# Ten instead of eight expert chunks loaded ahead of each layer's first expert product

## The chip, the cores and the metric

One core of a Trainium2 chip runs the kernel. The metric is the device time of one execution in microseconds. The kernel before took 2226.64 us, the median of three runs (2225.43 to 2228.95).

## What is computed

Two blocks of two layers each, on 256 tokens of width 1024, all in float32. The first block has a mixer (attention and pooling in layer 0, a short convolution in layer 1), a post norm, an expert-choice FFN and a post norm again. The expert FFN is the part that the change touches: 16 experts, each takes the 32 tokens that want it most.

```python
def _expert_choice_ffn(u, w_router, w_g, w_u, w_d):
    b, n, _ = u.shape
    cap = CAPACITY_FACTOR * n // N_EXPERTS
    logits = jnp.einsum('bnd,de->ben', u, w_router, preferred_element_type=jnp.float32)
    aff = jax.nn.softmax(logits, axis=1)
    gate, idx = lax.top_k(aff, cap)
    bidx = jnp.arange(b)[:, None, None]
    xe = u[bidx, idx]
    hg = jnp.einsum('becd,edf->becf', xe, w_g)
    hu = jnp.einsum('becd,edf->becf', xe, w_u)
    ye = jnp.einsum('becf,efd->becd', jax.nn.silu(hg) * hu, w_d) * gate[..., None].astype(u.dtype)
    return jnp.zeros_like(u).at[bidx, idx].add(ye)
```

The second block has three branches (two kinds of attention and a recurrence), projections and a merge. It uses neither experts nor the code of the change.

## The kernel before

All weights come through one stream of chunks. `weight_stream` (L238) fixes the order: the modulation's and mixer's chunks of layer 0, its 96 expert chunks, the convolution's and modulation's chunks of layer 1, its 96 expert chunks, then the second block's. A chunk is 128 partitions by 4096 floats, 2 MB. SyncE (SP) issues them all in this order, one DMA each (L625 to L648); the expert chunks come from a Fori loop of NG = 4 turns with 3 * KD = 24 chunks a turn (L633 to L638).

Each chunk has a place. `two_block_program` (L303) plans them: at first six slots, from chunk `widened` on WIDE = 8 slots in a fixed cycle, and for the second block RING = 4. Slots 0 to 3 lie in the tile `ring`, slots 4 to 7 in the upper part of `arena` (from column EXTRA = 7840). In the cycle they follow one another as ring, arena, arena, ring, and again. The planner records for every chunk the one that held the slot before (`occupant`) and what the slot's semaphore `weights_landed` has to reach (`arrived`). PE counts every chunk that it has used up in the semaphore `used`, in order. SP waits, before it issues chunk n, until `used` has passed the chunk that held the slot. So SP runs at most eight chunks ahead of PE.

An expert layer on PE is `ffn` (L1286). Its order in a layer:

- `post_norm(l, 0)` on DVE (L1967) makes h, with the norm's gain and offset in the tile `ln`; it signals `("h", l, 0, a)` for the two halves a of the tokens.
- PE turns h and multiplies with the router's weights: the signal `("logits", l)`. Its input `ut` lies in the arena's columns 4096 to 6143.
- DVE picks the 32 tokens of each expert, PE spreads the indices.
- Four groups of four experts. In each, PE gathers tokens (L1335), multiplies with 8 chunks of the gate weights, 8 of the up weights (L1339 to L1342), transposes (L1349), multiplies with 8 chunks of the down weights, and adds into the tokens' rows (L1362). `products` does a chunk: two halves of 512 columns times four experts, each expert on its own 32 columns of PE (L1324). `streamed` (L1316) waits for the chunk's semaphore.

PE's four groups are a Fori loop (L1330), as are those of ACT (L755) and POOL (L2499); DVE's are written out.

Rooms that the change uses: `ln` (2048 floats a partition: gain and offset), which POOL fills by `ln_params` (L2482) for each of the norms; `tab2`, the tables of the first block, whose first 2048 columns are the rotary tables, used by the mixer of layer 0 alone, and a part of the pooling's band; and the arena's columns 2048 to 6143, which hold the sum `acc` (first the norm's work tile), then `ht` and `ye` of the expert groups (L437). `acc` is first written at the end of a group, `ht` after its sixteenth chunk.

For the ln parameters of a layer's second norm POOL waits (L2546, L2551):

```python
            ln_params(0, 1, S("post_dve").at("h", 0, 0, 1))
            ln_params(1, 1, S("post_dve").at("h", 1, 0, 1))
```

They stand in POOL's program behind its own loop over the groups.

Of the kernel before, what the change touches and what calls it, by code (L numbers as in the profile page):

```python
# [31 lines left out]
D = 1024  # L32
KD = D // P
E = 16
CAP = 2 * T // E
EG = 4
NG = E // EG
HALF = 512
# [3 lines left out]
RING = 4  # L42
WIDE = 8
EARLY = (0, 1, 2, 3, 6, 7)
ARENA = 24832
SLOT = 8 * HALF
CH = 64
# [141 lines left out]
class Signal:  # L189
# [5 lines left out]
    def up(self, *key):  # L195

        self.value += 1
        self.marks[key] = self.value
        return self.handle, 1
# [103 lines left out]
def two_block_program(nc, w, out, marks, order):  # L303
    number = {key: n for n, (key, _) in enumerate(order)}
    widened = number[("mod", 0, 11)]
    narrowed = number[("in", 0, "rkv", 0)]
    place, arrived, occupant, latest = [], [], [], {}
    early = len(EARLY)
    wide = [s for s in range(WIDE) if s not in EARLY] + [EARLY[(widened + i) % early] for i in range(early)]
    for n, (key, _) in enumerate(order):  # L310
        if n < widened:
            place.append(EARLY[n % early])
        elif n < narrowed:
            place.append(wide[(n - widened) % WIDE])
        else:
            if n == narrowed:
                narrow = sorted(range(RING), key=lambda s: latest[s])
            place.append(narrow[(n - narrowed) % RING])
        before = latest.get(place[n])
        occupant.append(before)  # L320
        arrived.append((arrived[before] if before is not None else 0) + 16)
        latest[place[n]] = n
    view, starts, start = {}, [], 0
    for key, shape in order:
# [6 lines left out]
    with ExitStack() as ctx:  # L331
# [6 lines left out]
        h = h_t[:, :].rearrange("p (a d) -> p a d", a=TT)  # L338
        ln_t = sb("ln", 2 * D)
# [4 lines left out]
        tab2 = sb("tab2", max(n_first, n_second))  # L344
        par = sb("par", n_par)
        small_t = sb("small", 1152)
        arena = sb("arena", ARENA)
# [36 lines left out]
        def S(name):  # L384
            if name not in signals:
                handle = ctx.enter_context(nc.semaphore(name))
                signals[name] = Signal(handle, marks.setdefault(name, {}))
            return signals[name]


        landed = [ctx.enter_context(nc.semaphore(f"weights_landed{s}")) for s in range(WIDE)]
        used = ctx.enter_context(nc.semaphore("weights_used"))
        EXTRA = 7840

        def room(n, cols):

            s = place[n]
            if s < RING:
                return ring[:, s * SLOT:s * SLOT + cols]
            return arena[:, EXTRA + (s - RING) * SLOT:EXTRA + (s - RING) * SLOT + cols]  # L400

        def slot(key, *dims):
            k, n = view[key] or (EG, D)
# [6 lines left out]
        def consumed(key):  # L410

            return used, number[key] + 1
# [212 lines left out]
        @block.sync  # L625
        def _(sp):
            n = 0
            while n < len(order):
                key, shape = order[n]
                if key[0] == "expert":  # L630
                    layer = key[1]

                    with sp.Fori(0, NG) as g:  # L633
                        for m in range(3 * KD):
                            i = n + m
                            sp.wait_ge(used, g * (3 * KD) + (i - WIDE + 1))
                            sp.dma_start(room(i, EG * D), w["experts"][layer][bass.ds(g, 1), m].rearrange("a p c -> p (a c)")
                                         ).then_inc(landed[place[i]], 16)  # L638
                    n += 3 * KD * NG
                    continue  # L640
                if occupant[n] is not None:
                    sp.wait_ge(used, occupant[n] + 1)
                elif n >= widened:
                    sp.wait_ge(*consumed(("mix_in", 2)))
                    sp.wait_ge(*S("norm_dve").at("out", ("first", 2)))
                c = shape[0] * shape[1]
                sp.dma_start(room(n, c), w["stream"][starts[n]:starts[n] + P * c].rearrange("(p c) -> p c", p=P)
                             ).then_inc(landed[place[n]], 16)  # L648
                if key == ("mix_in", 0):
                    sp.dma_start(m0["uc"].rearrange("p k t -> p (k t)"), w["ctx_t"]).then_inc(loaded("ctx_t")[0], 16)  # L650
                if key == ("mix_in", 1):
                    sp.dma_start(tab2[:, 0:n_first], w["tables_first"]).then_inc(loaded("tables_first")[0], 16)
                n += 1
            for a in range(TT):
                sp.wait_ge(*S("second_dve").at("residual", 1, a))
                sp.dma_start(out[0, a * P:(a + 1) * P], h[:, a]).then_inc(loaded("result")[0], 16)
            sp.wait_ge(*loaded("result", TT))
# [360 lines left out]
        def _(pe):  # L1018
# [267 lines left out]
            def ffn(l):  # L1286
# [3 lines left out]
                for a in range(TT):  # L1290
# [4 lines left out]
                    mm = project(bank(0)[:, a * E:(a + 1) * E], lambda k: ff["ut"][:, k, a * P:(a + 1) * P], lambda k: router[:, k])  # L1295
# [18 lines left out]
                base = number[("expert", l, 0)]  # L1314

                def streamed(g, m, k):  # L1316
                    i = base + m * KD + k
                    pe.wait_ge(landed[place[i]], g * (16 * 3 * KD // WIDE) + arrived[i])
                    return room(i, EG * D).rearrange("p (e f) -> p e f", e=EG)

                def products(b, x, k, wk):
                    for half in range(2):
                        for e in range(EG):
                            mm = M(bank(b + half)[32 * e:32 * e + 32], x[:, k, 32 * e:32 * e + 32],  # L1324
                                   wk[:, e, half * HALF:(half + 1) * HALF], start=k == 0, stop=k == KD - 1,
                                   tile_position=(0, 32 * e))
                    return mm

                Sx.open_loop()
                with pe.Fori(0, NG) as g:  # L1330

                    pe.wait_ge(*Spl.turn(g, "pick"))
                    for k in range(KD):
                        for a in range(TT):
                            mm = M(bank(6 + k // 4)[:, k % 4 * P:k % 4 * P + P], h[:, a, k * P:(k + 1) * P], ff["pick_g"][:, a],  # L1335
                                   start=a == 0, stop=a == 1)
                        if k % 4 == 3:
                            mm.then_inc(*Sx.up("gather", k // 4))
                    pe.wait_ge(*Sax.turn(g, "xg", 3))  # L1339
                    pe.wait_ge(*Svx.turn(g, "xg", 7))  # L1340
                    for m in range(2):
                        for k in range(KD):  # L1342
                            mm = products(2 * m, ff["xg"], k, streamed(g, m, k))
                            mm.then_inc(used, 1)
                    for b in range(2):
                        pe.wait_ge(*Svx.turn(g, "hidden", b))
                        for i in range(4):
                            k = 4 * b + i
                            mm = nc.tensor.transpose(bank(6 + b)[:, i * P:(i + 1) * P], ff["hg"][:, k * P:(k + 1) * P],  # L1349
                                                     T1("ident"))  # L1350
                        mm.then_inc(*Sx.up("turned", b))
                    for k in range(KD):
                        if k % 4 == 0:
                            pe.wait_ge(*Sax.turn(g, "ht", k // 4))
                        mm = products(4, ff["ht"], k, streamed(g, 2, k))
                        mm.then_inc(used, 1)

                    for a in range(TT):
                        for half in range(2):
                            if a == 0:  # L1360
                                pe.wait_ge(*Svx.turn(g, "ye", half))
                            M(bank(2 * a + half), ff["put_g"][:, a * P:(a + 1) * P], ff["ye"][:, half * HALF:(half + 1) * HALF],  # L1362
                              start=True, stop=True).then_inc(*Sx.up("y", a, half))
                Sx.close_loop(NG)

            def second(l):
# [1104 lines left out]
        def _(po):  # L2471
# [10 lines left out]
            def ln_params(l, part, last):  # L2482
                if last is not None:
                    po.wait_ge(*last)
                for i, n in enumerate(("ln_mix_g", "ln_mix_b") if part == 0 else ("ln_ffn_g", "ln_ffn_b")):
                    po.dma_start(ln[:, i], w[n][l:l + 1, :].to_broadcast([P, D])).then_inc(loaded("ln")[0], 16)
# [56 lines left out]
            router(0)  # L2543
            gate_bias(1, 0)
            ffn(0)
            ln_params(0, 1, S("post_dve").at("h", 0, 0, 1))  # L2546
            gate_bias(1, 1)
            ln_params(1, 0, S("post_dve").at("h", 0, 1, 1))
            router(1)
            ffn(1)  # L2550
            ln_params(1, 1, S("post_dve").at("h", 1, 0, 1))  # L2551
            second(0)
            second(1)

# [45 lines left out]
```

## Time and profile before

| | |
|---|---|
| median of 3 runs | 2226.64 us (2225.43 to 2228.95) |
| the profiled execution | 2229.26 us, its span 2227.5 us |
| mean granted TensorE clock | 0.900 |
| PE busy, of the span | 1773.7 us (80%) |
| DVE, ACT, POOL busy | 569.0, 357.9, 57.6 us |
| moved by DMA | 586.61 MB, mean 263 GB/s |
| expert chunks | 192 of 2048 KB, issued by SP at L637 |

The span runs from the first to the last instruction of the program; the device time is 1.8 us longer. Busy times are sums over instructions. "PE" is the matmuls, "PEld" the weight loads, "SPq" the DMAs issued by SP. A timeline row merges instructions of one line: its start, the time to the end of the last one, the count behind x, and in brackets the idle time before it with what ended it. The x2 of a timeline row of SPq covers two issues; the second begins 0.33 us, the time of one issue, before the row's end.

### The profile page before, as it was taken

To read this page: it belongs to the slowest core of one execution; us is meant where nothing else is said; L and a number is where in the kernel's file an instruction comes from. 1 tells how busy PE (TensorE), PEld (TensorE's weight loads), DVE (VectorE), ACT (ScalarE), POOL (GpSimd) and SP (SyncE) were. 2 spreads that over 40 slices of the span, in tenths; PEclk is the share of its full clock that TensorE was granted. 3 is DMA by queue.
4 is the path that set the end of the run, shared out by engine and by line. 5 is a ranking of instruction groups with operands and counts; after the bars stand their busy time and mean duration, and the time that the engine had idled before them with its cause. 6 is when DMAs were issued, how large, how long until landed. Compare 5 with 4: busy or idle time off the path is not lost. (4 is left out here: it accounts for less than half of the span.)

```text
span 2227.5 us, 27241 instructions
## 1 busy us (share of the span) xinstructions
PE 1773.7 (80%) x11768; PEld 1050.5 (47%) x11768; DVE 569.0 (26%) x1125; ACT 357.9 (16%) x721; POOL 57.6 (3%) x69
## 2 busy tenths in 40 slices
PE   6897765656568977656665679999999999999999
PEld 4454220211117842112111167787578678775775
DVE  0434010100007640001000035332343242414432
ACT  1231000000000010000000013313431122324310
POOL 0000000000000000000000001010000001100000
PEclk9997787888879977878787789999999999999999
DMA  9892899999999928999999943112423232113221
GB/s 405 354 381 85 353 428 428 428 428 428 428 428 425 393 102 362 428 428 428 428 428 422 428 177 144 71 61 85 151 76 114 102 135 77 71 63 118 110 91 43
DMA packets 43502, 586.61 MB, mean 263 GB/s; under 512 B 4912, under 2 KB 5040, under 8 KB 8080
## 3 DMA queue, kind: packets, MB, share of 16 engines
q1 hardware_dynamic: 40464, 574.18, 62.6%
q0 software_dynamic: 2224, 8.32, 0.9%
q10 hardware_dynamic: 720, 2.74, 0.3%
q8 instruction: 73, 1.20, 0.2%
q14 instruction: 21, 0.17, 0.0%
HBM read 584.17 MB, written 1.05 MB: 263 GB/s over the span
## 5 line engine op out<-in xcount | busy, mean ns | idle before, releaser
L1324 PE MATMUL ps<-ring,arena 128*32 128x512 f32 x1536 | 251.5, 789 | 180.2 <-DMA ring<-in_experts 167.4
L1324 PE MATMUL ps<-arena 128*32 128x512 f32 x1536 | 244.1, 771 | 154.0 <-DMA arena<-in_experts 154.0
L1090 PE MATMUL ps<-arena,ring 128*128 128x256 f32 (+3 forms) x1248 | 236.9, 351 | 9.2 <-DVE arena L1870 2.6
L1090 PEld LDWEIGHTS ps<-arena,ring 128*128 128x128 f32 (+2 forms) x1248 | 206.0, 191 | 38.5 <-ACT arena L685 6.1
L1324 PEld LDWEIGHTS ps<-ring,arena 128*32 128x32 f32 x1536 | 49.5, 128 | 362.9 <-DMA ring<-in_experts 228.0
L1324 PEld LDWEIGHTS ps<-arena 128*32 128x32 f32 x1536 | 49.1, 126 | 348.7 <-DMA arena<-in_experts 257.7
L1420 PE MATMUL ps<-arena,ring 128*128 128x256 f32 x768 | 183.5, 388 | 0.0
L1420 PEld LDWEIGHTS ps<-arena,ring 128*128 128x128 f32 x768 | 142.9, 191 | 29.1 <-issue 9.7
L1443 PE MATMUL ps<-arena,ring 128*128 128x256 f32 x640 | 152.0, 389 | 0.0
L2099 DVE TENSOR_TENSOR arena<-ps,arena 128x512 f32<-128x512 f32 x16 | 10.3, 686 | 499.4 <-PE ps L1324 499.4
L1443 PEld LDWEIGHTS ps<-arena,ring 128*128 128x128 f32 x640 | 124.1, 195 | 27.3 <-issue 10.1
L1090 PE MATMUL ps<-arena 128*128 128x256 f32 (+2 forms) x416 | 102.2, 406 | 4.5 <-ACT arena L985 2.5
L1090 PEld LDWEIGHTS ps<-arena 128*128 128x128 f32 x416 | 76.1, 196 | 30.2 <-issue 16.7
L2103 DVE TENSOR_TENSOR arena<-ps,gate 128x512 f32<-128x512 f32 x16 | 10.3, 686 | 300.0 <-PE ps L1324 300.0
L764 ACT ACTIVATE arena<-ps 128x512 f32<-128x512 f32 x16 | 9.5, 597 | 308.2 <-PE ps L1349 308.2
L758 ACT ACTIVATE arena<-ps,modcol 128x128 f32<-128x128 f32 x32 | 12.1, 457 | 277.7 <-PE ps L1335 277.7
L1743 PE MATMUL ps<-ring,ln 128*128 128x512 f32 x128 | 55.3, 592 | 0.0
L761 ACT ACTIVATE arena<-ps 128x1024 f32<-128x1024 f32 x8 | 8.2, 1024 | 221.9 <-PE ps L1324 221.9
L965 ACT ACTIVATE arena<-arena 128x128 f32<-128x128 f32 x64 | 28.6, 448 | 91.7 <-DVE arena L2413 91.7
L1055 PE MATMUL ps<-ring,arena 128*32 128x512 f32 x176 | 26.4, 734 | 20.2 <-DMA tab<-in_tables 15.8
L1090 PE MATMUL ps<-ring,arena 128*128 128x512 f32 x96 | 42.3, 593 | 0.0
L2243 DVE TENSOR_TENSOR arena<-arena,ps 128x512 f32<-128x512 f32 (+1 forms) x40 | 25.4, 635 | 61.1 <-PE ps L1542 61.0
(337 smaller groups left out, 1900.9 us busy)
## 6 DMA issues: line engine op xcount, KB each, us to landing
ring<-in_experts SPq DMA_DIRECT2D x96, 2048.0 KB, 35.6
arena<-in_experts SPq DMA_DIRECT2D x96, 2048.0 KB, 35.8
ring<-in_stream SPq DMA_DIRECT2D x61, 2048.0 KB, 8.6
arena<-in_stream SPq DMA_DIRECT2D x15, 2048.0 KB, 21.1
ring<-in_stream SPq DMA_DIRECT2D x2, 1728.0 KB, 7.0
gate<-in_b_mod POOLq DMA_DIRECT2D x4, 512.0 KB, 10.9
ring<-in_stream SPq DMA_DIRECT2D x4, 512.0 KB, 3.6
tab<-in_tables_first SPq DMA_DIRECT2D x1, 1729.0 KB, 42.5
```

The source lines that it names most:

```text
L758: A(ff["xg"][:, k], bank(6)[:, k * P:(k + 1) * P], ACT.Identity, scale=modcol[:, l, 3, k, 0:1], bias=modcol[:, l, 2, k, 0:1]).then_inc(*Sx ...
L764: A(ff["ht"][:, 4 * b:4 * b + 4], bank(6 + b).rearrange("p (k n) -> p k n", k=4), ACT.Copy).then_inc(*Sx.up("ht", b))
L965: A(at2["prob"][:, u % 2, o:o + n], at2["score"][:, u % 2, o:o + n], ACT.Exp, bias=st[:, 4 * (u % 2) + a:4 * (u % 2) + a + 1], accum_out=s ...
L1055: mm = M(bank(mod_bank((l, j)))[o:o + 32], md["condT"][:, k], slot(key)[:, k], start=k < 4, stop=k >= 4, tile_position=(0, o))
L1090: mm = M(dst, lhs(k), rhs(k), start=k == 0, stop=k == n - 1)
L1324: mm = M(bank(b + half)[32 * e:32 * e + 32], x[:, k, 32 * e:32 * e + 32], wk[:, e, half * HALF:(half + 1) * HALF], start=k == 0, stop=k == ...
L1420: mm = M(bank(fill_bank(n))[:, x * T:x * T + T], slot(key)[:, k, c:c + P], s2["ht"][:, k], start=k == 0, stop=k == KD - 1)
L1443: mm = M(bank(fill_bank(n))[:, x * T:x * T + T], slot(key)[:, k, c:c + P], s2["ht"][:, k], start=k == 0, stop=k == KD - 1)
L1743: mm = M(bank(2 * a + j), merged[:, k, a * P:(a + 1) * P], slot(key)[:, k], start=k == 0, stop=k == KD - 1)
L2099: V.tensor_tensor(ff["hg"][:, b * HALF:(b + 1) * HALF], bank(2 + b), ff["hg"][:, b * HALF:(b + 1) * HALF], ALU.mult).then_inc(*up("hidden" ...
L2103: V.tensor_tensor(ff["ye"][:, b * HALF:(b + 1) * HALF], bank(4 + b), gate[:, 1, b * HALF:(b + 1) * HALF], ALU.mult).then_inc(*up("ye", b))
L2243: V.tensor_tensor(m, m, bank(hh)[:, x * 256:], ALU.subtract).then_inc(*Sv.up("inv", *K, n, hh))
```

## The change

Two rooms are added to the eight slots, with semaphores of their own, each used once a layer. Place 8 (HALVED) takes expert chunk 8 in two halves: columns 0 to 2047 of the chunk into `ln`, 2048 to 4095 into `tab2`. Place 9 (WHOLE) takes chunk 9 into the arena's columns 2048 to 6143. The other 94 expert chunks of a layer, and all after them, go round the eight slots as before. SP waits for the second h of the layer's first post norm before chunk 8, and for the logits before chunk 9. POOL's load of the second norm's parameters waits for chunk 8 to be used. The loops over groups on SP and PE are written out, since the chunks' places are no longer the same in each turn.

```diff
+HALVED, WHOLE = WIDE, WIDE + 1
...
+        elif key[0] == "expert" and key[2] in (WIDE, WIDE + 1):
+            place.append(HALVED if key[2] == WIDE else WHOLE)
         elif n < narrowed:
-            place.append(wide[(n - widened) % WIDE])
+            place.append(wide[rounds % WIDE])
+            rounds += 1
...
-        arrived.append((arrived[before] if before is not None else 0) + 16)
+        arrived.append((arrived[before] if before is not None else 0) + (32 if place[n] == HALVED else 16))
...
-        landed = [ctx.enter_context(nc.semaphore(f"weights_landed{s}")) for s in range(WIDE)]
+        landed = [ctx.enter_context(nc.semaphore(f"weights_landed{s}")) for s in range(WIDE + 2)]
...
             s = place[n]
+            if s == WHOLE:
+                return arena[:, 2048:2048 + cols]
...
+        def halves_of(n):
+
+            return (ln_t[:, 0:2 * D], tab2[:, 0:2 * D])
...
-                if key[0] == "expert":
-                    layer = key[1]
-
-                    with sp.Fori(0, NG) as g:
-                        for m in range(3 * KD):
-                            i = n + m
-                            sp.wait_ge(used, g * (3 * KD) + (i - WIDE + 1))
-                            sp.dma_start(room(i, EG * D), w["experts"][layer][bass.ds(g, 1), m].rearrange("a p c -> p (a c)")
-                                         ).then_inc(landed[place[i]], 16)
-                    n += 3 * KD * NG
-                    continue
                 if occupant[n] is not None:
                     sp.wait_ge(used, occupant[n] + 1)
...
+                if key[0] == "expert":
+                    _, layer, s = key
+                    src = w["experts"][layer][s // (3 * KD), s % (3 * KD)]
+                    if place[n] == HALVED:
+                        sp.wait_ge(*S("post_dve").at("h", layer, 0, 1))
+                        for i, part in enumerate(halves_of(n)):
+                            sp.dma_start(part, src[:, i * 2 * D:(i + 1) * 2 * D]).then_inc(landed[HALVED], 16)
+                    else:
+                        if place[n] == WHOLE:
+                            sp.wait_ge(*S("ffn_pe").at("logits", layer))
+                        sp.dma_start(room(n, EG * D), src).then_inc(landed[place[n]], 16)
+                    n += 1
+                    continue
...
                 def streamed(g, m, k):
-                    i = base + m * KD + k
-                    pe.wait_ge(landed[place[i]], g * (16 * 3 * KD // WIDE) + arrived[i])
-                    return room(i, EG * D).rearrange("p (e f) -> p e f", e=EG)
+
+                    i = base + (3 * g + m) * KD + k
+                    pe.wait_ge(landed[place[i]], arrived[i])
+                    parts_of = halves_of(i) if place[i] == HALVED else (room(i, EG * D)[:, 0:2 * D], room(i, EG * D)[:, 2 * D:])
+                    return lambda e, f: parts_of[e // 2][:, e % 2 * D + f * HALF:e % 2 * D + (f + 1) * HALF]
...
-                with pe.Fori(0, NG) as g:
-
+                for g in range(NG):
+                    up = Sx.again if g else Sx.up
...
-            ln_params(0, 1, S("post_dve").at("h", 0, 0, 1))
+            ln_params(0, 1, consumed(("expert", 0, WIDE)))
...
-            ln_params(1, 1, S("post_dve").at("h", 1, 0, 1))
+            ln_params(1, 1, consumed(("expert", 1, WIDE)))
```

On SP, from the last chunk ahead of layer 0's experts (L647) into the loop over them, before (an ISA row is a wait):

```order
L647 DMA ring<-in_stream 128x4096 [waits weights_used]
L633 UNCONDITIONAL_BRANCH
L633 ISA
L637 ISA [waits weights_used]
L637 DMA ring<-in_experts 128x4096
L636 REGISTER_ALU
L637 ISA [waits weights_used]
L637 DMA arena<-in_experts 128x4096
```

The same place with the change, from the last chunk ahead of the experts (L659) on:

```order
L659 DMA ring<-in_stream 128x4096 [waits weights_used]
L655 DMA ring<-in_experts 128x4096 [waits weights_used]
L655 DMA arena<-in_experts 128x4096 [waits weights_used] x2
L655 DMA ring<-in_experts 128x4096 [waits weights_used] x2
L655 DMA arena<-in_experts 128x4096 [waits weights_used] x2
L655 DMA ring<-in_experts 128x4096 [waits weights_used]
L651 DMA ln<-in_experts 128x2048 [waits post_dve,norm_dve,weights_used]
L651 DMA tab<-in_experts 128x2048
L655 DMA arena<-in_experts 128x4096 [waits ffn_pe,norm_dve,weights_used]
L655 DMA ring<-in_experts 128x4096 [waits weights_used]
```

Three DMAs for the two chunks now stand behind the first eight expert chunks, ahead of the first chunk that takes over a slot from an expert chunk, and no register work is left.

On PE, the products of chunks 7 to 10 of the first group, before (L1324):

```order
L1324 MATMUL ps<-ring,arena 32x512 [waits weights_landed0]
L1324 MATMUL ps<-ring,arena 32x512 x7
L1324 MATMUL ps<-ring,arena 32x512 [waits weights_landed1]
L1324 MATMUL ps<-ring,arena 32x512 x7
L1318 REGISTER_ALU
L1324 MATMUL ps<-arena 32x512 [waits weights_landed4]
L1324 MATMUL ps<-arena 32x512 x7
```

And with the change (L1338):

```order
L1338 MATMUL ps<-ring,arena 32x512 [waits weights_landed0]
L1338 MATMUL ps<-ring,arena 32x512 x7
L1338 MATMUL ps<-ln,arena 32x512 [waits weights_landed8]
L1338 MATMUL ps<-ln,arena 32x512
L1338 MATMUL ps<-tab,arena 32x512 x2
L1338 MATMUL ps<-ln,arena 32x512 x2
L1338 MATMUL ps<-tab,arena 32x512 x2
L1338 MATMUL ps<-arena 32x512 [waits weights_landed9]
L1338 MATMUL ps<-arena 32x512 x7
L1338 MATMUL ps<-ring,arena 32x512 [waits weights_landed1]
```

Chunk 8 is read from `ln` and `tab2` by turns, chunk 9 from the arena, and chunk 10 takes the slot that chunk 8 had. The products are the same in number and shape.

## Rows read from the trace of the kernel before

**Rows 1.** Page: busy time, then tenths and GB/s in 40 slices of 55.7 us.
```profile
PE 1773.7 (80%) x11768; PEld 1050.5 (47%) x11768; DVE 569.0 (26%) x1125; ACT 357.9 (16%) x721; POOL 57.6 (3%) x69
...
PE   6897765656568977656665679999999999999999
...
DMA  9892899999999928999999943112423232113221
GB/s 405 354 381 85 353 428 428 428 428 428 428 428 425 393 102 362 428 428 428 428 428 422 428 177 144 71 61 85 151 76 114 102 135 77 71 63 118 110 91 43
```

**Rows 2.** Busy time by stretch: length, PE, PEld, DVE, ACT, POOL, PEclk, DMA share, GB/s.
```profile
165.00:228.00 63.00, 49.09 (x163) 31.58 (x161) 26.74 (x61) 9.58 (x21) 0.93 (x2) 0.76 0.21 75
228.00:246.00 18.00, 16.97 (x156) 5.17 (x160) 0.93 (x3) 1.02 (x1) 0.19 (x1) 1.00 0.79 319
246.00:671.00 425.00, 255.22 (x1536) 62.70 (x1528) 22.24 (x36) 21.34 (x30) 2.81 (x8) 0.81 1.01 428
...
699.00:777.00 78.00, 76.49 (x365) 65.96 (x363) 55.12 (x102) 2.42 (x8) 0.00 (x0) 1.00 0.99 405
777.00:840.00 63.00, 48.20 (x164) 30.31 (x164) 27.25 (x62) 9.57 (x21) 0.40 (x1) 0.78 0.28 104
...
858.00:1288.00 430.00, 256.96 (x1528) 63.12 (x1528) 22.24 (x36) 21.35 (x30) 4.90 (x12) 0.80 1.01 427
1288.00:1312.00 24.00, 15.78 (x88) 12.91 (x88) 15.01 (x28) 6.46 (x20) 0.00 (x0) 0.79 0.41 173
1312.00:1500.00 188.00, 180.86 (x2230) 152.57 (x2231) 71.59 (x115) 49.32 (x86) 22.41 (x17) 1.00 0.26 95
```

**Rows 3.** Timeline of PE in layer 0's experts: chunks 0 to 2, 10, 22, 23, 71.
```profile
228.65 1.92 PE L1324 MATMUL ps<-ring,arena 128*32 128x512 f32 x16 [1.54 <-DVE arena L2091]
230.38 3.62 PE L1324 MATMUL ps<-arena 128*32 128x512 f32 x32
233.82 3.62 PE L1324 MATMUL ps<-ring,arena 128*32 128x512 f32 x32
...
249.59 3.15 PE L1324 MATMUL ps<-arena 128*32 128x512 f32 x16 [2.98 <-DMA arena<-in_experts]
...
308.36 3.50 PE L1324 MATMUL ps<-arena 128*32 128x512 f32 x16 [2.98 <-DMA arena<-in_experts]
313.26 1.92 PE L1324 MATMUL ps<-ring,arena 128*32 128x512 f32 x16 [1.40 <-DMA ring<-in_experts]
...
548.38 1.92 PE L1324 MATMUL ps<-ring,arena 128*32 128x512 f32 x16 [1.38 <-DMA ring<-in_experts]
```

**Rows 4.** Timeline of SP's DMA issues: chunks 7 and 8 of layer 0, of layer 1.
```profile
192.14 38.96 SPq L637 DMA_DIRECT2D ring<-in_experts  x2
...
804.84 37.70 SPq L637 DMA_DIRECT2D ring<-in_experts  x2
```

**Rows 5.** Timeline of PE: chunk 95 of layer 0, of layer 1.
```profile
668.46 1.92 PE L1324 MATMUL ps<-ring,arena 128*32 128x512 f32 x16 [1.50 <-DMA ring<-in_experts]
...
1284.05 3.37 PE L1324 MATMUL ps<-ring,arena 128*32 128x512 f32 x16 [2.97 <-DMA ring<-in_experts]
```

**Rows 6.** Timelines of DVE and PE: second h; logits of both layers; layer 1's first product.
```profile
196.94 1.28 DVE L2006 SCALAR_TENSOR_TENSOR h<-arena,ln 128x1024 f32<-128x1024 f32 x1
...
202.64 3.57 PE L1090 MATMUL ps<-small,arena 128*128 128x16 f32 x16 [1.55 <-DVE arena L1872]
...
814.50 3.57 PE L1090 MATMUL ps<-small,arena 128*128 128x16 f32 x16 [1.55 <-DVE arena L1872]
...
840.09 1.92 PE L1324 MATMUL ps<-ring,arena 128*32 128x512 f32 x16 [1.54 <-DVE arena L2091]
```

**Rows 7.** DMA issues from 165 to 228 us: count, KB, us from issue to landing.
```profile
ring<-in_experts SPq DMA_DIRECT2D x1, 2048.0 KB, 8.4
```

**Rows 8.** Instruction queue: packets, MB, share; whole span, then 300 to 314 us.
```profile
q8 instruction: 73, 1.20, 0.2%
...
q8 instruction: 1, 0.02, 0.5%
```

More of the change, by code:

```diff
@@ L307, in two_block_program @@
     place, arrived, occupant, latest = [], [], [], {}
-    early = len(EARLY)
+    early, rounds = len(EARLY), 0
     wide = [s for s in range(WIDE) if s not in EARLY] + [EARLY[(widened + i) % early] for i in range(early)]
@@ L1324, in products @@
                             mm = M(bank(b + half)[32 * e:32 * e + 32], x[:, k, 32 * e:32 * e + 32],
-                                   wk[:, e, half * HALF:(half + 1) * HALF], start=k == 0, stop=k == KD - 1,
+                                   wk(e, half), start=k == 0, stop=k == KD - 1,
                                    tile_position=(0, 32 * e))
@@ L1337, in ffn @@
                         if k % 4 == 3:
-                            mm.then_inc(*Sx.up("gather", k // 4))
+                            mm.then_inc(*up("gather", k // 4))
                     pe.wait_ge(*Sax.turn(g, "xg", 3))
@@ L1350, in ffn @@
                                                      T1("ident"))
-                        mm.then_inc(*Sx.up("turned", b))
+                        mm.then_inc(*up("turned", b))
                     for k in range(KD):
@@ L1362, in ffn @@
                             M(bank(2 * a + half), ff["put_g"][:, a * P:(a + 1) * P], ff["ye"][:, half * HALF:(half + 1) * HALF],
-                              start=True, stop=True).then_inc(*Sx.up("y", a, half))
+                              start=True, stop=True).then_inc(*up("y", a, half))
                 Sx.close_loop(NG)
```

## The prediction

> **What bounds the kernel now.** I read the page first. PE is busy 80% of the span, but the line of slices shows two regimes [rows 1]: up to about slice 24 DMA moves 428 GB/s in most slices and PE stands at 6 or 7 tenths; after it PE is at 9 and DMA at 60 to 150 GB/s. So the first 1290 us are bound by transfers wherever transfers run, and the rest by PE. The change touches only the first part.
>
> Next, busy time by stretch, one row per stage [rows 2]. The two expert stretches (246 to 671 and 858 to 1288 us) run at 428 and 427 GB/s while PE works only 60% of them. In between lie the stretches that matter here: 165 to 228 us at 75 GB/s and 777 to 840 us at 104 GB/s. There the norm, the router and the choice of tokens run, all eight slots are full or still held, and the DMA queues stand still. What is not moved there is moved later, when every chunk costs time.
>
> PE's timeline gives the price of a chunk [rows 3]. In steady state each chunk's 16 matmuls (8 products, in two passes each) start when the chunk lands: the releaser is a DMA, and PE was idle for 1.4 to 3.0 us before. Chunk 10 starts at 249.59 and chunk 71 at 548.38: 61 steps in 298.79 us, 4.90 us each. PE needs 1.72 us for a chunk when it is there (two chunks from 230.38 to 233.82). Two pauses between expert groups lie in this stretch and do not disturb it, because eight slots carry the queue over them.
>
> The queue of SP gives the start of the race [rows 4]. Chunk 7 of layer 0 is issued at 192.14. The next issue, chunk 8, comes at the end of that pair, 192.14 + 38.96 - 0.33 = 230.77, when PE has used chunk 0, whose products start at 228.65 [rows 3]. In layer 1 it is 804.84 and 842.21. From there until the last chunk the DMA never rests, and the last product waits for it: 668.46 in layer 0 and 1284.05 in layer 1 [rows 5]. Behind it come the last y products, then the post norm, all waiting for that product.
>
> **The change part by part.** *Two chunks more before the first product.* Chunk 8 goes in two halves into the norm parameters' room and the lower part of the first tables' room, chunk 9 into the arena over the sum. Chunk 8 waits on SP for the second h of the post norm, which ends at 196.94 + 1.28 = 198.22 in layer 0; chunk 9, behind it, for the router's logits, at 202.64 + 3.57 = 206.21 in layer 0 and 814.50 + 3.57 = 818.07 in layer 1 [rows 6]. Chunk 7, issued in this quiet stretch, landed 8.4 us later [rows 7]. Chunk 9 is therefore there at about 214.6 and 826.5, 14 us before the first products at 228.65 and 840.09 [rows 3, 6]. The two transfers cost nothing: they fill stretches that run at 75 and 104 GB/s [rows 2]. If that cover were gone, each would cost its 4.90 us, and the change would give nothing.
>
> *What stands behind the two waits on SP.* Only chunk 10 and later. Chunk 10 needs the slot of chunk 0, which is free only after the first product, later than h and logits. So nothing is held up.
>
> *The race afterwards.* Chunk 10 is now issued when chunk 8 was, 230.8, and lands when chunk 8 did. PE eats chunks 0 to 11 without a pause (12 x 1.72 = 20.6 us from 228.65, to 249.3), and chunk 12 lands at the place of chunk 10, 249.59. Chunk 18 is the first to wait for a slot used late: chunk 10 is used by 228.65 + 11 x 1.72 = 247.6, while the queue holds work until about 231 + 8 x 4.90 = 270. The DMA does not starve. From chunk 12 every chunk starts two steps, 2 x 4.90 = 9.80 us, earlier. **Gain: 9.80 us per layer, 19.6 us in all.** Per chunk I keep 4.8 to 5.0 as bounds, 19.2 to 20.0.
>
> *What carries it to the end.* All that follows an expert stage hangs on its last product: after layer 0 the conv's chunks follow in the same queue and PE works without a break from 699 to 777 (76.5 of 78 us) [rows 2], and SP's later issues wait for used chunks, so all of it moves as one. The small loads of the last turn (ln_ffn, tables of the second block, on POOL's queue) stay on the same turn: their waits lie behind POOL's own loop, where h and chunk 8 are both long done. They cost the same as before.
>
> *Slots of the following stages.* The slots turn by two per layer, four in all. The pattern ring, arena, arena, ring repeats after four, so the second block's first four chunks again take over the slots of expert chunks 88, 91, 92 and 95. No earlier, no later.
>
> *Loops written out on PE and SP.* The register work and jumps go. They lie in stretches where PE waits 1.4 to 3.0 us for every chunk [rows 3], so they cost nothing now and give nothing when they go.
>
> *More code to fetch.* This is the new cost. Matmuls and loads together, the four turns of layer 0 show 156 + 1536 and 160 + 1528 [rows 2], 845 instructions a turn. Three more turns in each of two layers are about 5070. The page has 11768 + 11768 executed [rows 1]; less the 5070 repeated ones, 18466 came in 73 packets of the instruction queue [rows 8], 253 each: the change adds **20 packets** of 16 KB. One was fetched between 300 and 314 us, beside a full queue [rows 8], and the chunks there start at 308.36 and 313.26, 4.90 us apart [rows 3]. I take zero, since that is the one row of the very thing. The other bound: a packet holds one of the 16 DMA engines for 16384 B / (428 GB/s / 16) = 0.61 us, and if all 20 fell on one engine that every chunk waits for, 12.2 us. The Trainium skill, DMA: Bandwidth & Descriptors, section Queues, rings and completion order, says that each DMA engine takes turns between the queues it has work for, packet by packet; by that rule a fetch always takes its time from the stream, the sum would go toward the second bound, and the one fetch looked at here shows no such loss.
>
> *Clock.* At the few places where PE alone is on the path, its level matters: the last product of layer 1 takes 3.37 us, that of layer 0 1.92 [rows 5]. I count about six such joins, at 1.45 us each way and not all at once, and allow 3 us either way.
>
> **Sum.** -19.6 +- 0.4 for the chunks, 0 for fetches, 0 +- 3 for the joins. The profiled execution took 2229.26 us (span 2227.5); it would become 2209.7, span 2207.9. The median shown is 2226.64, so I predict **2207.0 us**.
>
> **Rivals.**
> *A, instruction packets slow the stream.* For it: 20 packets, nearly all in the saturated stretches, and a chunk counts only when all of it is there. Against: the undisturbed step at the fetch after 300 us [rows 3, 8]. Price 12.2: 2226.6 - 19.6 + 12.2 = 2219.2. Chance 0.06.
>
> *B, one extra chunk is late.* If chunk 9 landed after PE asks for it, or its slot's wait were longer than the trace shows, only one chunk per layer counts: -9.8, 2216.8. The 14 us of margin speak against. Chance 0.03.
>
> *C, slower: the second block starts at a low clock.* From 1312 us PE is the bound to the end, 915 us. It runs at granted 1.00, but enters from a stretch at 0.79, and the quiet stretches stand at 0.76 and 0.78 [rows 2]. At the lower of its two levels (1.2 instead of 2.4 GHz) work takes up to twice as long, as the two last products show [rows 5]. The sign turns once 39 us there run at the lower level; 52 us would cost 26 and give 2226.6 - 19.6 + 26 = 2233.0. Nothing in the change alters what PE does before 1312, only when. Chance 0.02.
>
> *D, the change does nothing:* some wait elsewhere sets the time of layer ends. The releasers say DMA up to the last product [rows 5], so 0.02, at 2226.6.
>
> **Chances.** The forecast has 0.87. Faster by over 0.2% (4.5 us, about what a measurement tells from no change): forecast, A and B, 0.95 rounded; within: 0.03; slower: 0.02. The range of the forecast is 2203 to 2211; I widen it toward A and B, and a little down for lucky joins: 2202 to 2214.
>
> **What would show it.** Right: first product of layer 0 still at 228.6; DMA issues into ln, tab and arena near 198 and 206; twelve chunks without a pause, then the wait before chunk 12 at 249.6; steps of 4.90; last products at 658.7 and 1264.4; granted clock and PE busy after the experts as before. A would show as steps above 4.90 at each fetch; B as a pause before chunk 9; C as a low clock behind 1293. Wrong: steady steps longer than 4.97, or an expert stage that is not two steps shorter.

## The result, and the profile after

| | before | after |
|---|---|---|
| median, us | 2226.66 (2225.43 to 2228.95, 4 runs) | 2208.82 (2202.30 to 2210.55, 4 runs) |
| profiled execution, us | 2229.26 | 2202.30 |
| its span, us | 2227.5 | 2200.5 |
| mean granted clock | 0.900 | 0.902 |

The ratio is 0.9912, with a 95% interval from 0.9894 to 0.9929. The forecast was 2207.0, in a range from 2202 to 2214. The profiled execution of after is the shortest of its runs; what that means for the reading comes below.

The page of after: busy time, the slices of PE and DMA, GB/s, and the instruction queue (its packets, MB and share). The answers of before are [rows 1, 8].

```profile
PE 1762.1 (80%) x11768; PEld 1047.0 (48%) x11768; DVE 568.8 (26%) x1125; ACT 357.5 (16%) x721; POOL 57.5 (3%) x69
...
DMA  9894899999999948999999942112323332213320
GB/s 407 361 386 162 368 428 427 427 427 428 427 427 422 380 163 373 427 428 427 428 427 423 428 168 116 72 62 86 153 77 115 123 117 78 72 63 115 115 98 37
...
q8 instruction: 93, 1.52, 0.3%
```

The fourth slice moves 162 GB/s where it moved 85 and the fifteenth 163 where it moved 102. The instruction counts of all engines are what they were. The instruction queue has exactly the 20 packets more that were worked out.

Busy time of after by stretch (length, PE, PEld, DVE, ACT, POOL, PEclk, DMA share, GB/s), to be held against [rows 2]:

```profile
165.00:228.00 63.00, 47.87 (x195) 29.95 (x197) 27.66 (x63) 9.57 (x21) 1.11 (x3) 0.78 0.39 146
246.00:661.00 415.00, 255.92 (x1495) 63.47 (x1487) 22.98 (x37) 21.33 (x30) 2.79 (x8) 0.78 1.01 427
...
767.00:830.00 63.00, 48.13 (x178) 30.16 (x180) 27.25 (x62) 9.57 (x21) 0.40 (x1) 0.78 0.43 161
848.00:1268.00 420.00, 250.97 (x1515) 64.09 (x1508) 22.98 (x37) 21.34 (x30) 4.87 (x12) 0.80 1.01 427
...
1292.00:1480.00 188.00, 180.41 (x2226) 151.95 (x2225) 71.30 (x114) 49.28 (x86) 22.38 (x17) 1.00 0.26 95
```

The stretch from 165 to 228 moves 71 GB/s more than before, which over 63 us is 4.5 MB: two chunks of 2.1 MB, and the start of chunk 10, which is issued at 226.00 here. The expert stretches are as full as before, and PE behind them runs at a granted 1.00 again.

SP's queue in after (start, duration, what is issued), against [rows 4]:

```profile
194.54 0.33 SPq L651 DMA_DIRECT2D ln<-in_experts  x1
194.91 0.43 SPq L651 DMA_DIRECT2D tab<-in_experts  x1
201.69 0.33 SPq L655 DMA_DIRECT2D arena<-in_experts  x1
226.00 0.33 SPq L655 DMA_DIRECT2D ring<-in_experts  x1
...
799.59 0.33 SPq L651 DMA_DIRECT2D ln<-in_experts  x1
806.74 24.22 SPq L655 DMA_DIRECT2D arena<-in_experts  x2
```

Chunk 8 goes out in its two halves, chunk 9 follows 7 us later, and then the queue rests until 226.00, when chunk 10 may take the slot of chunk 0. In layer 1 it is the same (the last row holds chunks 9 and 10).

PE in after (start, duration, operation, number of instructions, and in brackets the idle time ahead with its releaser): chunk 0, chunk 1 with 2, two pieces of chunk 8, chunks 11, 12 and 13, chunk 95, and the first and last products of layer 1. Against [rows 3, 5, 6]:

```profile
224.02 1.92 PE L1338 MATMUL ps<-ring,arena 128*32 128x512 f32 x16 [1.51 <-issue]
225.74 3.64 PE L1338 MATMUL ps<-arena 128*32 128x512 f32 x32
...
237.75 0.63 PE L1338 MATMUL ps<-ln,arena 128*32 128x512 f32 x2
237.79 0.60 PE L1338 MATMUL ps<-tab,arena 128*32 128x512 f32 x2
...
242.91 1.93 PE L1338 MATMUL ps<-arena 128*32 128x512 f32 x16
245.01 1.92 PE L1338 MATMUL ps<-arena 128*32 128x512 f32 x16 [0.17 <-DMA arena<-in_experts]
249.91 3.64 PE L1338 MATMUL ps<-ring,arena 128*32 128x512 f32 x16 [2.98 <-DMA ring<-in_experts]
...
655.56 3.40 PE L1338 MATMUL ps<-arena 128*32 128x512 f32 x16 [1.25 <-DMA arena<-in_experts]
...
828.65 1.92 PE L1338 MATMUL ps<-arena 128*32 128x512 f32 x16 [1.51 <-issue]
...
1264.07 1.92 PE L1338 MATMUL ps<-ring,arena 128*32 128x512 f32 x16 [1.36 <-DMA ring<-in_experts]
```

Chunks 8 and 9 are there when PE asks. Chunk 12 is the first that comes late, by 0.17 us, 20.99 us after the first product; from then on PE waits for the chunks, as it did from chunk 10 before. Only behind each pause between two groups are a few there in advance (in both kernels).

**Where the time went.** I cut each profiled execution at four starts of products: chunk 0 and chunk 95 in each layer. The table has the same cuts for every execution that was profiled, us. *Front* is up to layer 0's first product, *join* from layer 0's chunk 95 to layer 1's first product, *tail* from layer 1's chunk 95 to the end.

| kernel | front | layer 0 | join | layer 1 | tail | span |
|---|---|---|---|---|---|---|
| before | 228.65 | 439.81 | 171.63 | 443.96 | 943.43 | 2227.5 |
| before, again (r_before) | 224.34 | 439.82 | 171.64 | 443.86 | 941.66 | 2221.3 |
| after | 224.02 | 431.53 | 173.10 | 435.42 | 936.42 | 2200.5 |
| after, again (r_after) | 223.84 | 431.56 | 173.05 | 435.48 | 941.83 | 2205.8 |
| e1_written_out | 221.98 | 441.22 | 176.68 | 445.42 | 942.34 | 2227.6 |
| e2_nine | 228.3 | 436.19 | 174.92 | 440.44 | 943.82 | 2223.7 |
| e3_late | 223.08 | 440.91 | 176.48 | 446.13 | 941.47 | 2228.1 |
| e4_looped | 223.17 | 429.76 | 174.17 | 434.29 | 941.18 | 2202.6 |
| e4_again | 221.96 | 430.13 | 174.19 | 434.16 | 941.42 | 2201.9 |
| e5_padded | 223.74 | 435.38 | 175.86 | 439.66 | 941.08 | 2215.7 |

Two executions of one kernel agree in the two layers within 0.4 us and in the join within 0.1. Front and tail don't: two executions of before have fronts of 228.65 and 224.34, two of after have tails of 936.42 and 941.83. So layers and join are read from single profiles, and front and tail are not. For that reason the 27.0 us between the first two spans overstate the change. The two profiles taken on one chip, r_after and r_before, differ by 15.5: 8.3 and 8.4 less in the layers, 1.4 more in the join, 0.5 less in front and 0.2 more in the tail.

The two tails of after differ in the granted clock. Some 319 us behind layer 1's chunk 95 (1264.07 and 1263.94 us) the profiled execution of after has

```profile
1583.00:1591.00 8.00, 6.04 (x34) 5.14 (x35) 4.46 (x16) 3.65 (x14) 0.00 (x0) 1.00 0.24 100
```

and r_after, which is the same kernel,

```profile
1583.00:1591.00 8.00, 6.76 (x21) 5.65 (x22) 3.13 (x12) 2.46 (x9) 0.00 (x0) 0.57 0.14 59
```

In these 8 us r_after does 21 matmuls where after does 34. From 1290 us to the end the mean granted clock is 1.00 in after and 0.99 in r_after.

### The profile page after: what moved, and what is told of

It reads as the page before. It is cut to its first block and busy times, and to the rows that moved or that the text cites. A ratio compares the mean times of both kernels' runs of the same rounds, so it can differ in the third digit from the quotient of the medians.

```text
span 2200.5 us, 26521 instructions
## 1 busy us (share of the span) xinstructions
PE 1762.1 (80%) x11768; PEld 1047.0 (48%) x11768; DVE 568.8 (26%) x1125; ACT 357.5 (16%) x721; POOL 57.5 (3%) x69
## 5 line engine op out<-in xcount | busy, mean ns | idle before, releaser
L1338 PE MATMUL ps<-arena 128*32 128x512 f32 x1536 | 243.3, 766 | 170.3 <-DMA arena<-in_experts 164.1
L1338 PE MATMUL ps<-ring,arena 128*32 128x512 f32 x1504 | 247.7, 793 | 147.9 <-DMA ring<-in_experts 141.7
L1338 PEld LDWEIGHTS ps<-arena 128*32 128x32 f32 x1536 | 50.7, 125 | 347.2 <-DMA arena<-in_experts 235.4
L1338 PEld LDWEIGHTS ps<-ring,arena 128*32 128x32 f32 x1504 | 50.9, 130 | 338.3 <-DMA ring<-in_experts 223.4
L1434 PE MATMUL ps<-arena,ring 128*128 128x256 f32 x768 | 182.7, 387 | 0.0
L1457 PE MATMUL ps<-arena,ring 128*128 128x256 f32 x640 | 147.7, 381 | 0.0
L1067 PE MATMUL ps<-ring,arena 128*32 128x512 f32 x176 | 25.2, 704 | 19.5 <-DMA tab<-in_tables 14.9
```

The costliest lines, as they stand in the source:

```text
L1067: mm = M(bank(mod_bank((l, j)))[o:o + 32], md["condT"][:, k], slot(key)[:, k], start=k < 4, stop=k >= 4, tile_position=(0, o))
L1434: mm = M(bank(fill_bank(n))[:, x * T:x * T + T], slot(key)[:, k, c:c + P], s2["ht"][:, k], start=k == 0, stop=k == KD - 1)
L1457: mm = M(bank(fill_bank(n))[:, x * T:x * T + T], slot(key)[:, k, c:c + P], s2["ht"][:, k], start=k == 0, stop=k == KD - 1)
```

## The experiments

There are eight runs. Two of them are of kernels unaltered, r_after and r_before; the others are of edits of after. Ratios are to before, whose runs on the two chips had medians of 2226.80 (21 runs) and 2227.54 (11 runs).

**e1_written_out: the loops written out, but eight chunks ahead.**

```diff
-        elif key[0] == "expert" and key[2] in (WIDE, WIDE + 1):
+        elif False:
...
-            ln_params(0, 1, consumed(("expert", 0, WIDE)))
+            ln_params(0, 1, S("post_dve").at("h", 0, 0, 1))
...
-            ln_params(1, 1, consumed(("expert", 1, WIDE)))
+            ln_params(1, 1, S("post_dve").at("h", 1, 0, 1))
```

> The change's loops written out on PE and SP, but eight chunks ahead as before. It tells what the writing out does by itself. Theory 1 (the gain comes from the two early chunks, jumps and fetches cost nothing): same time as the kernel before, 2226.7 within 3 us; the stretch from the start of chunk 10 to that of chunk 95 stays 418.9 us in layer 0. Theory 2 (each of the 20 added instruction packets holds the stream for up to 0.61 us): those stretches grow by 1 to 6 us per layer and the time by 2 to 12 us. Theory 3 (the gain comes from the jumps that are gone): the time falls by most of 18 us.

Measured: 2232.28 (2229.44 to 2235.06, 7 runs), ratio 1.0028 (1.0017 to 1.0039). Slower than before, by a little, and clearly so. This is the second of the three theories: it gave 2 to 12 us in all and 1 to 6 us per layer. The instruction queue has 93 packets, as in after. The layers are 1.41 and 1.46 us longer than before, the join 5.05. So the two chunks ahead are what gains: after less e1 is -9.69 in layer 0 and -10.00 in layer 1, for 2 x 4.90 = 9.80 worked out. And writing the loops out is not free.

PE in e1 has the loss at one place in layer 0. These are two chunks of the third of the four turns (g = 2, chunks 48 to 71), and chunk 95:

```profile
508.14 2.71 PE L1338 MATMUL ps<-ring,arena 128*32 128x512 f32 x16
513.67 3.36 PE L1338 MATMUL ps<-arena 128*32 128x512 f32 x16 [2.82 <-DMA arena<-in_experts]
...
663.20 3.53 PE L1338 MATMUL ps<-ring,arena 128*32 128x512 f32 x16 [2.97 <-DMA ring<-in_experts]
```

The start at 513.67 comes 5.53 us after the one before, released by a DMA, where the step is 4.90. The 5.05 us of the join are of another kind, and the windows behind chunk 95 of before and of e1 show most of them. Before:

```profile
668.46:699.06 30.60, 23.39 (x167) 19.20 (x168) 21.80 (x37) 3.60 (x10) 2.11 (x4) 0.94 1.01 425
```

e1:

```profile
663.20:697.70 34.50, 27.36 (x167) 21.57 (x168) 21.91 (x37) 3.59 (x10) 2.10 (x4) 0.80 1.01 425
```

The same 167 matmuls take 3.97 us longer at a granted 0.80 instead of 0.94, and chunk 95 itself runs at the lower level of the clock (3.53 us, where [rows 5] has 1.92). PE had been waiting for chunks ahead of both. Three kernels were profiled twice (before, after, and e4 below), and their joins repeat within 0.1 us; between kernels the join differs by up to 5.05.

**e2_nine: only the halved chunk ahead, nine in all.**

```diff
-        elif key[0] == "expert" and key[2] in (WIDE, WIDE + 1):
+        elif key[0] == "expert" and key[2] == WIDE:
```

> Only chunk 8 goes to a room of its own (in halves); chunk 9 takes its turn in the eight slots: nine ahead. Theory 1: half of the chunks, half of the gain: 9.8 us less than before plus whatever the written out loops cost, so about 2217 to 2219, and one layer's stretch from first product to last product is 4.9 us shorter. If the gain came from something else than the number of chunks ahead, it would be all there or gone.

Measured: 2221.17 (2216.97 to 2225.47, 7 runs), ratio 0.9972 (0.9960 to 0.9984). The median lies 2.2 us above the 2217 to 2219 that were expected; the layers, below, are as expected. SP issues chunk 8 early and then nothing until chunk 0 is used:

```profile
197.98 0.33 SPq L651 DMA_DIRECT2D ln<-in_experts  x1
...
230.27 0.33 SPq L655 DMA_DIRECT2D ring<-in_experts  x1
```

Chunk 11 now stands where chunk 10 stood, 20.59 us after the first product (20.94 in before):

```profile
248.88 1.92 PE L1338 MATMUL ps<-arena 128*32 128x512 f32 x16 [1.49 <-DMA arena<-in_experts]
```

The layers are 5.03 and 4.98 us shorter than e1's, and after's are 4.66 and 5.02 shorter than e2's. Each chunk is worth one step of the stream, the first like the second.

**e3_late: both rooms used, but loaded only when chunk 0 has been used.**

```diff
                         sp.wait_ge(*S("post_dve").at("h", layer, 0, 1))
+                        sp.wait_ge(*consumed(("expert", layer, 0)))
```

> The change, but SP issues chunk 8 only when chunk 0 is used (chunks 9 and 10 right behind it). Ten chunks of room, none of them filled in the quiet stretch. Theory 1 (what counts is that the transfers run in the quiet stretch): no gain, 2226.7 plus the cost of the written out loops, 2225 to 2232. Rival (more slots, a deeper queue or the order of slots bring the gain): as fast as the change, about 2209.

Measured: 2228.62 (2225.37 to 2235.19, 12 runs), ratio 1.0011 (1.0001 to 1.0021). SP in e3 around the first product:

```profile
225.12 0.33 SPq L652 DMA_DIRECT2D ln<-in_experts  x1
...
226.03 0.36 SPq L656 DMA_DIRECT2D arena<-in_experts  x1
226.44 0.72 SPq L656 DMA_DIRECT2D ring<-in_experts  x1
```

Chunks 8, 9 and 10 go out together behind the first product, and PE waits for chunk 10 as in before:

```profile
243.54 3.22 PE L1339 MATMUL ps<-ring,arena 128*32 128x512 f32 x16 [2.98 <-DMA ring<-in_experts]
```

The layers are 9.38 and 10.71 us longer than after's, and within 0.8 of e1's. Ten chunks' room with eight chunks ahead of the first product gains nothing: what counts is bytes moved while the queues would rest, not buffers.

**e4_looped and e4_again: ten chunks ahead, and PE's last three turns a loop again.** SP keeps its written-out issues.

```diff
-                    i = base + (3 * g + m) * KD + k
-                    pe.wait_ge(landed[place[i]], arrived[i])
+                    if isinstance(g, int):
+                        i = base + (3 * g + m) * KD + k
+                        pe.wait_ge(landed[place[i]], arrived[i])
+                    else:
+                        i = base + (3 + m) * KD + k
+                        pe.wait_ge(landed[place[i]], g * (16 * 3 * KD // WIDE)
+                                   + (arrived[i] - 16 * 3 * KD // WIDE))
...
-                for g in range(NG):
-                    up = Sx.again if g else Sx.up
+                def turn_of(g, up):
...
+                turn_of(0, Sx.up)
+                with pe.Fori(1, NG) as g:
+                    turn_of(g, Sx.again)
```

> The change, with PE's turns 1 to 3 as a loop again (turn 0 written out, since its chunks' places differ). It saves about 13 of the 20 added instruction packets. Theory 1 with fetches free: as the change, 2208.8 within 2 us. Theory 2 (fetches slow the stream a little): 1 to 3 us faster than the change, and the steps of 4.9 us are without the slips that the change shows, such as 5.74 and 5.60 at 500 us.

> The change with PE's turns 1 to 3 as a loop, again, now timed on the same chip as the change itself. If the added instruction packets cost the stream 1.5 us a layer, it is 2 to 4 us faster than the change; if they cost nothing, the two are equal within 1 us.

Measured: e4_looped 2205.18 (2203.34 to 2209.75, 5 runs), ratio 0.9907 (0.9895 to 0.9920); e4_again, the same kernel beside r_after, 2207.38 (2203.70 to 2208.27, 5 runs), ratio 0.9910 (0.9896 to 0.9925). The page of e4_looped:

```profile
q8 instruction: 79, 1.29, 0.2%
```

14 of the 20 packets are gone. The layers are 1.4 to 1.8 and 1.1 to 1.3 us shorter than after's, and against before (10.05 and 9.67 in e4_looped) they have the whole of the 9.80 worked out. The place is the third turn again. PE in after:

```profile
494.79 3.57 PE L1338 MATMUL ps<-arena 128*32 128x512 f32 x16 [2.98 <-DMA arena<-in_experts]
500.53 1.92 PE L1338 MATMUL ps<-arena 128*32 128x512 f32 x16
506.13 3.64 PE L1338 MATMUL ps<-ring,arena 128*32 128x512 f32 x16 [3.67 <-DMA ring<-in_experts]
511.01 3.64 PE L1338 MATMUL ps<-ring,arena 128*32 128x512 f32 x16 [1.25 <-DMA ring<-in_experts]
```

The same chunks in e4_looped:

```profile
493.64 3.43 PE L1342 MATMUL ps<-arena 128*32 128x512 f32 x16 [2.98 <-DMA arena<-in_experts]
499.23 1.92 PE L1342 MATMUL ps<-arena 128*32 128x512 f32 x16
503.43 3.58 PE L1342 MATMUL ps<-ring,arena 128*32 128x512 f32 x16 [2.27 <-DMA ring<-in_experts]
508.33 1.92 PE L1342 MATMUL ps<-ring,arena 128*32 128x512 f32 x16 [1.32 <-DMA ring<-in_experts]
```

Three steps take 508.33 - 493.64 = 14.69 us with the loop, which is 3 x 4.90, and 511.01 - 494.79 = 16.22 written out. The third of these chunks (chunk 65) lands late, by 1.5 us, and all that follows keeps the delay. As a whole e4 beats before as clearly as after does; over after its lead shows in the layers, while the intervals of the ratios overlap.

**r_after: after, unaltered, beside e4_again.**

> The changed kernel again, unaltered, for its spread and a second profile. Expected: 2205 to 2212; in the profile 434 and 437 us from first to last product of the two layers as before, with the join between the layers and the stretches ahead and behind different by up to 4 us each, since those hang on the clock granted there.

Measured: 2210.36 (2203.29 to 2212.70, 6 runs), ratio 0.9919 (0.9902 to 0.9936). It confirms the result in another set of runs, and the layers to 0.06 us. (The 434 and 437 us of the expectation, and the 441.1 and 446.3 of r_before's, are counted to the start of chunk 95's last matmul, where the table counts to its first. So counted the layers are 434.1 and 436.8 here, 441.2 and 446.1 in r_before.)

**e5_padded: each wait for a chunk repeated in turns 1 to 3.** 52 further waits on the same value stand behind each of the first. If packets take time from the stream, more of them should take more.

```diff
-                    pe.wait_ge(landed[place[i]], arrived[i])
+                    for _ in range(53 if g else 1):
+                        pe.wait_ge(landed[place[i]], arrived[i])
```

> The change with 26 further instructions ahead of each chunk's products in turns 1 to 3 of both layers (waits on a semaphore that has long its value, they hold nothing up): 3744 instructions, 15 more packets, 7 a layer, between the same products. If packets fetched beside the full queue cost 0.15 us each, as 10 more did 1.5 us a layer, the expert stages grow by 1 us each; if each holds its DMA engine for 0.61 us and no slack is left, by 4 us each; if the 1.5 us of the written out loops had another cause, by nothing. Above 5 us a stage the inserted instructions themselves would be the cause, and PE would show no idle time ahead of a chunk.

Measured: 2217.86 (2214.93 to 2219.00, 4 runs), ratio 0.9954 (0.9936 to 0.9972). PE issued 26 further waits per chunk (3744 instructions more), and the page has

```profile
q8 instruction: 107, 1.75, 0.3%
```

The layers are 3.85 and 4.24 us longer than after's. PE's timeline of e5 puts a part of that on the waits themselves:

```profile
345.13 1.92 PE L1339 MATMUL ps<-arena 128*32 128x512 f32 x16 [1.66 <-issue]
349.99 2.63 PE L1339 MATMUL ps<-ring,arena 128*32 128x512 f32 x16 [2.94 <-issue]
```

What ends the idle time is now PE's own issue, not a DMA. So the waits do hold PE up, which the expectation had denied. How much, layer 0's chunk 95 shows: its issue by SP, the time from issue to landing, and the start of its products:

```profile
622.66 0.33 SPq L655 DMA_DIRECT2D arena<-in_experts  x1
...
arena<-in_experts SPq DMA_DIRECT2D x1, 2048.0 KB, 33.5
...
659.11 3.64 PE L1339 MATMUL ps<-arena 128*32 128x512 f32 x16 [2.08 <-issue]
```

It landed at 622.66 + 33.5 = 656.2 and was used 2.9 us later; in layer 1 (1238.95 + 32.8, and 1274.64) it is the same. In the other kernels chunk 95's products start within 0.1 us of its landing. These 2.9 us are the second cost of e5. They stand once in a layer's time, because every late chunk of the turns g = 1 to 3 is used that much later.

What is left is the stream's. To have it alone, I take the time from the start of chunk 14, whose products wait for its landing in every kernel and which still lies in the first turn (g = 0), to the landing of chunk 95, and count the packets of the instruction queue in it:

| kernels | packets, layer 0 and 1 | layer 0, us | layer 1, us |
|---|---|---|---|
| before, r_before | 2, 1 | 399.27, 399.47 | 403.45, 403.37 |
| e4_looped, e4_again | 5, 5 | 399.27, 399.88 | 403.91, 403.81 |
| after, r_after, e1, e2, e3 | 12, 11 | 400.76 to 401.43 | 404.94 to 405.40 |
| e5_padded | 19, 19 | 402.2 | 406.6 |

The queue of data was as full in e5 as elsewhere, so PE's late use did not starve it:

```profile
254.00:656.00 402.00, 240.95 (x1448) 67.16 (x1448) 21.69 (x35) 21.36 (x30) 2.80 (x8) 0.80 1.01 427
```

The time grows with the packets in both layers: by 1.4 to 2.1 us for 10 more than the mean of before's two profiles has, by 2.8 and 3.2 us for 17 and 18 more. That is 0.14 to 0.21 us a packet, an estimate from these rows; 3 and 4 more (e4) cost 0.2 and 0.5 us on the mean. With the 2.9 us, and a chunk 14 that lands 0.5 and 0.3 us earlier behind the first product in e5, this makes up the 3.85 and 4.24 us. The price does not come evenly. By pieces of layer 0, e5 and after are both 1.5 us longer than before from chunk 47 to 71; from 71 to 95 e5 is 1.3 longer, and after not at all. So e5 agrees with the first of its three expected prices (0.15 us each) and not with the third (nothing). What it can't tell is why one chunk is delayed by over a microsecond and its neighbours by nothing.

**r_before: before, unaltered, one profiled execution on the chip of r_after.**

> The kernel before again, for a second profile: expert stages of 441.1 and 446.3 us from first to last product within 0.5 us, the join between the layers anywhere from 170 to 174 us.

Measured: 2223.11 us, span 2221.3. PE's chunk 0 and chunk 95 in layer 0:

```profile
224.34 1.92 PE L1324 MATMUL ps<-ring,arena 128*32 128x512 f32 x16 [1.54 <-DVE arena L2091]
...
664.16 1.92 PE L1324 MATMUL ps<-ring,arena 128*32 128x512 f32 x16 [1.50 <-DMA ring<-in_experts]
```

The first product is at 224.34 here and at 228.65 in [rows 3], with the same kernel. The 4.6 us by which after's first product came earlier than that of before are therefore not the change's.

## Why the prediction was right, step by step

- **Two chunks, 9.80 us a layer: right.** e1, e2 and after are three points on one line: eight, nine and ten chunks ahead, at steps of 5.03 and 4.66 us in layer 0 and 4.98 and 5.02 in layer 1. The row behind the term was the steady step of 4.90 [rows 3].
- **Hidden in the quiet stretch: right.** e3 has the buffers without the cover, and the whole gain is gone, as the prediction said of that case.
- **Nothing held up behind the two waits on SP: right.** Chunk 10 goes out 1.98 us after the first product starts (224.02, 226.00), as chunk 8 did before (228.65, 230.77).
- **Twelve chunks without a pause, then the wait before chunk 12: right.** Chunk 12 starts 20.99 us after the first product (245.01 - 224.02); 20.94 were foretold (249.59 - 228.65).
- **Loops written out worth nothing, fetches taken at zero: this term was mis-sized.** The prediction had both ends, 0 and 12.2 us, and took 0 because one fetch had been seen beside an undisturbed step. The number of packets was right (73 + 20 = 93). The cost is 1.41 and 1.46 us in the layers by e1, 2.9 in all, and going back to the loop on PE removed it (e4). One undisturbed fetch showed that a fetch need not delay a chunk, and not that 20 wouldn't: the delays come at one or two chunks of a layer, so a single fetch is no measure. Rival A had the mechanism, and 9.3 of its 12.2 us did not come; the estimate of 0.61 us a packet is some three to four times the 0.14 to 0.21 that e5's table gives.
- **Joins, 0 +- 3 us: right.** The one between the layers gave +1.5: chunk 95 of layer 0 takes 3.40 us where it took 1.92. Chunk 95 of layer 1 went the other way, 1.92 for 3.37.
- **Rivals B, C and D** fell: no extra chunk is late, the second block runs at a granted 1.00 behind 1292 us, and the layers are shorter.

The sum by its terms: -19.6 for the chunks, +2.9 for the code, +1.4 for the join, -15.3 us. The profiles of one chip say -15.5. The medians say -17.8 and -17.2, with intervals of the ratio some 4 us to each side; the 2 us between terms and medians lie within them, and cannot be placed. By the measured terms the forecast should have been 2211.3. That the median came within 1.8 us of 2207.0 is in part luck; that it lies in the range is not.

## What to carry to other kernels

When a stage is bound by transfers and the stretch ahead of it leaves the queues at rest, every chunk landed in that stretch is worth one steady step of the stream, and nothing more; look for rooms that are dead just then, and check the wait that frees them against the first use. A buffer that can only be filled once the stage runs gains nothing. If the slots' pattern breaks a loop, write out the turn that differs and keep the rest a loop: copies of code have a price beside a full stream. Here it was 0.14 to 0.21 us for each added packet of 16 KB, known only on the mean: look at a whole stage, not at one fetch.

## What the hardware showed that was not expected

- **Instruction packets delay a full stream, at one or two chunks of a layer.** The written-out kernels (after, e1, e2, e3, e5 and r_after) take 201.7 to 202.5 us from chunk 30 to chunk 71; with a loop on PE (before, e4) it is 200.7 to 200.9. Nearly all of the loss stands behind chunk 47: from 30 to 47 all kernels have 83.2 to 83.5 us, from 47 to 71 118.4 to 119.1 written out and 117.5 to 117.6 with the loop. From 312 to 406 us after and e4_looped fetch three packets each and lose nothing. From 429 to 548 us after fetches four and e4_looped none, and there after loses its 1.5 us; from 549 to 655 it is three to none, and no loss (r_after has 0.6 us of its loss there). Why a chunk is late there and not elsewhere stays open. The Trainium skill, DMA: Bandwidth & Descriptors, section Queues, rings and completion order, has each DMA engine take turns between its queues packet by packet, so that each fetch takes time from the stream. The totals agree with its direction (e5's table), at 0.14 to 0.21 us a packet; no view here shows the engines one by one, and the size and the jumps stay unexplained.
- **Turns of a loop are not fetched again.** In e4_looped no packet of the instruction queue comes between 440 and 655 us, while PE runs a body of some 845 matmuls and loads for the second and third time.
- **The clock at the end of a stage repeats for a kernel.** The joins of one kernel repeat within 0.1 us (three kernels, two profiles each), and between kernels they go from 171.6 to 176.7. Writing out the loops alone (e1) moved the join by 5.05 us, of which 3.9 stand where the granted clock was 0.80 instead of 0.94. What sets the level is not shown. It is as large as many a change one would like to measure, so a small edit should be judged by the stages it touches as well as by the total.
